# A mixture of experts that streams its weights: w1 and w3 loaded in halves for every pair, the second pair by quarters, and a late gather spread otherwise

## The reference

```python
def hier_moe(h, w_grp, b_grp, w_exp, b_exp, w1, w3, w2):
...
    w = pg_top * pe_top / jnp.sum(pe_top, axis=-1, keepdims=True)
    eid = g_sel * EXP_PER_GROUP + e_sel
    combine = jnp.sum(jax.nn.one_hot(eid, N_EXPERTS, dtype=f32) * w[..., None], axis=1)
    hid = jax.nn.silu(jnp.einsum('td,edf->tef', t, w1)) * jnp.einsum('td,edf->tef', t, w3)
    hid = hid * combine[..., None].astype(hid.dtype)
    out = jnp.einsum('tef,efd->td', hid, w2)
```

## Time and profile before

| | us |
|---|---|
| median of 3 runs | 1208.77 (1208.54 to 1209.69) |
| the profiled execution | 1207.29 |
| its span | 1205.5 |
| PE busy | 1173.3 (97%) |
| DVE busy | 700.5 (58%) |
| ACT busy | 379.0 (31%) |
| read from HBM | 334.97 MB |

### The profile page before, as it was taken

One profiled execution on the slowest core, in us unless ns is written; L12 is line 12 of the kernel. 1 busy time (PEld: TensorE's weight loads), 2 busy tenths in 40 slices (PEclk: granted clock), 3 DMA queues, 4 the chain that ended last, 5 costly groups with the idle time before them and its releaser, 6 DMA issues.

```text
span 1205.5 us, 18956 instructions
## 1 busy us (share of the span) xinstructions
PE 1173.3 (97%) x7316; PEld 886.3 (74%) x7316; DVE 700.5 (58%) x1024; ACT 379.0 (31%) x406; POOL 44.9 (4%) x53
## 2 busy tenths in 40 slices
PE   8999999999999999999999999999999999999995
PEld 8888888888888888888898888655555454545552
DVE  5778555556566767676886656444444444434445
ACT  5444433334444353543434543100101110000103
POOL 1000001001002022000000000000000000000002
PEclk9999999999999999999999999999999999999998
DMA  8665565765855555455664896999999999999996
GB/s 301 194 194 189 180 201 177 203 198 176 215 171 158 169 174 162 153 174 178 204 211 116 277 403 259 350 417 432 431 432 432 430 432 429 434 431 431 425 418 247
DMA packets 161707, 337.70 MB, mean 280 GB/s; under 512 B 13552, under 2 KB 139648, under 8 KB 148352
## 3 DMA queue, kind: packets, MB, share of 16 engines
q1 hardware_dynamic: 154544, 335.69, 75.8%
q10 hardware_dynamic: 7120, 1.42, 0.6%
HBM read 334.97 MB, written 2.12 MB: 280 GB/s over the span
## 4 chain that ended last, share of the span: by engine, by line
PE 82%; DMA 14%; DVE 1%; issue 1%; SPq 0%; ACT 0%; POOL 0%; POOLq 0%; DVEq 0%; ACTq 0%
PE ps L1056 20%; PE ps L1405 14%; DMA w_b<-in_w_dram 14%; PE ps L1086 12%; PE ps L1059 10%; PE ps L1089 6%; PE ps L1214 4%; PE ps L1437 4%; PE ps L1216 2%; PE ps L1446 2%; PE ps L1339 1%; PE ps L1447 1%; PE ps L1031 1%; PE ps L1178 0%; DMA xin<-in_x_dram 0%
## 5 line engine op out<-in xcount | busy, mean ns | idle before, releaser
L1533 DVE TENSOR_TENSOR wsplit<-wraw,wsplit 128x2048 fp32r<-128x2048 f32 x119 | 273.6, 2299 | 176.2 <-ACT wsplit L724 176.1
L724 ACT ACTIVATE wsplit<-wraw 128x2048 fp32r<-128x2048 f32 x119 | 228.1, 1917 | 368.3 <-PE ps L1059 194.1
L1056 PE MATMUL ps<-act_split,wsplit 128*128 128x512 f32 x1024 | 323.2, 397 | 0.0
L1405 PE MATMUL ps<-w_a,xe_a 128*64 128x256 f32 x960 | 219.8, 385 | 12.5 <-DMA w_b<-in_w_dram 12.2
L1059 PEld LDWEIGHTS ps<-act_split,wsplit 128*128 128x128 f32 x1024 | 192.4, 188 | 45.4
L1405 PE MATMUL ps<-w_b,xe_b 128*64 128x256 f32 x960 | 219.9, 385 | 0.0
L1405 PEld LDWEIGHTS ps<-w_a,xe_a 128*64 128x64 f32 x960 | 129.8, 138 | 98.1 <-DMA w_b<-in_w_dram 21.0
L1059 PE MATMUL ps<-act_split,wsplit 128*128 128x256 f32 x1024 | 201.3, 278 | 0.0
L1086 PE MATMUL ps<-wsplit,act_split 128*128 128x512 f32 x608 | 191.9, 397 | 0.0
L1056 PEld LDWEIGHTS ps<-act_split,wsplit 128*128 128x128 f32 x1024 | 156.4, 189 | 0.9 <-issue 0.4
L1089 PEld LDWEIGHTS ps<-wsplit,act_split 128*128 128x128 f32 x608 | 114.2, 188 | 26.9
(11 more groups left out here) (315 smaller groups left out, 1127.3 us busy)
## 6 DMA issues: line engine op xcount, KB each, us to landing
wraw<-in_w_in_dram SPq DMA_DIRECT2D x88, 1024.0 KB, 5.1
w_a<-in_w_dram SPq DMA_DIRECT2D x37, 2048.0 KB, 15.4
w_b<-in_w_dram SPq DMA_DIRECT2D x37, 2048.0 KB, 19.5
wraw<-in_w_out_dram SPq DMA_DIRECT2D x16, 1024.0 KB, 6.5
w_a<-in_w_dram SPq DMA_DIRECT2D x14, 1024.0 KB, 12.7
w_b<-in_w_dram SPq DMA_DIRECT2D x14, 1024.0 KB, 15.1
wraw<-in_w_branch_m_dram SPq DMA_DIRECT2D x8, 1024.0 KB, 5.1
wraw<-in_w_branch_a_dram SPq DMA_DIRECT2D x8, 1024.0 KB, 5.2
```

Of the source, the lines that this page charges most:

```text
L724: act.activation(wsplit[:, q % 2, :, 0], wraw[:, q % RAW], ACT.Copy).then_inc(rounded, 1)
L1056: pe.matmul(banks[b], w[:, k, 0, b * P:(b + 1) * P], act_of(q, k), start=first and k == 0, stop=False)
L1405: last = pe.matmul(ps[b * SLOTS:(b + 1) * SLOTS, 2 * w, 0:FF], operands[b][:, k], w13[b][:, w, k], start=k == 0, stop=k == DC - 1)
L1533: dve.tensor_tensor(wsplit[:, q % 2, :, 1], wraw[:, q % RAW], wsplit[:, q % 2, :, 0].bitcast(F32), ALU.subtract).then_inc(split, 1)
```

## The change

SP loads w1 and w3 of pairs 2 to 13 in halves of 1.05 MB, each after the part that used it, so eight loads a pair instead of four. Pair 1's come in quarters of 0.52 MB, 16 of them, released at the middle and the end of each of pair 0's parts (a new semaphore `mid_parts` in place of `first_quarter`). Each part on PE waits for its own half. PE's loop over pairs of pairs has its first pass written out.

The late gather's banks stand otherwise between pair 0's parts: one bank after each of the first two parts, two after each of the others, and the last two behind the turn, where it was 2, 2, 2, 1 and one behind the turn. On ACT the eviction of bank 6 moves behind the copy of the turned tile, and on DVE `up(0)` moves ahead of bank 5.

```diff
-                    for w, w_v in enumerate((w1_v, w3_v)):
-                        parts_done(i, 2 * w + 1)
+                    for part in range(PARTS):
+                        w, h = divmod(part, 2)
+                        ks = slice(h * PART_K, (h + 1) * PART_K)
+                        parts_done(i, part)
                         for b in range(2):
-                            sp.dma_start(w13[b][:, w], w_v[:, ds(i * 2 + b, 1)]).then_inc(w13_loaded[w][0], 16)
+                            sp.dma_start(w13[b][:, w, ks], (w1_v, w3_v)[w][:, ds(i * 2 + b, 1), ks]).then_inc(w13_loaded[w][h], 16)
...
-                sp.wait_ge(first_quarter, chunks)
-                for b in range(2):
-                    load_steps(b, 2 + b, 0, 0, DC // 4, w13_loaded[0][0])
-                parts_done(1, 0)
-                for b in range(2):
-                    load_steps(b, 2 + b, 0, DC // 4, DC // 2, w13_loaded[0][0])
-                for part in range(1, PARTS):
-                    parts_done(1, part)
-                    for b in range(2):
-                        load_part(b, 2 + b, part)
+                for part in range(PARTS):
+                    w, h = divmod(part, 2)
+                    for quarter in range(2):
+                        if quarter == 0:
+                            sp.wait_ge(mid_parts, (chunks - 1) * PARTS + (part + 1))
+                        else:
+                            parts_done(1, part)
+                        first = (2 * h + quarter) * (DC // 4)
+                        for b in range(2):
+                            load_steps(b, 2 + b, w, first, first + DC // 4, w13_loaded[w][h])
...
-                    gathered(1, (2, 4, 6))
+                    gathered(1, (2, 4))
                     turn_hidden(0)
+                    gathered(1, (6,))
...
-                    second_halves = {0: 32, LAST - 1: 96, LAST: 128}.get(i, 64) if isinstance(i, int) else 64
-                    quarters = 32 if w == 0 and not (isinstance(i, int) and i == 0) else 0
-                    pe.wait_ge(w13_loaded[w][h], second_halves if h else i * 32 + (32 + quarters))
+                    quarters = 0 if isinstance(i, int) and i == 0 else 32
+                    pe.wait_ge(w13_loaded[w][h], i * 32 + (32 + quarters))
...
-                        if isinstance(i, int) and i == 0 and part == 0 and k == DC // 4 - 1:
-                            last.then_inc(first_quarter, 1)
+                        if isinstance(i, int) and i == 0 and k % (DC // 2) == DC // 4 - 1:
+                            last.then_inc(mid_parts, 1)
...
-                hidden(0, 0, (xg[:, :, 0:SLOTS], xe_first), [[lambda js=js: gather_late(js)] for js in ((0, 1), (2, 3), (4, 5), (6,))])
+                hidden(0, 0, (xg[:, :, 0:SLOTS], xe_first), [[lambda js=js: gather_late(js)] for js in ((0,), (1,), (2, 3), (4, 5))])
                 turn(0)
-                gather_late((7,))
+                gather_late((6, 7))
...
-                with pe.Fori(0, N_PAIRS // 2 - 2) as j:
+                hidden_and_scatter(1, 0)
+                rows(0, 1, 1)
+                hidden_and_scatter(2, 1)
+                rows(1, 2, 0)
+                with pe.Fori(1, N_PAIRS // 2 - 2) as j:
...
                 make_x2(*late_chunks[0])
+                up(0)
+                starts_at = starts_of(1, 0)
                 gathered(1, (5,))
                 make_x2(*late_chunks[1])
-                up(0)
-                starts_at = starts_of(1, 0)
                 gathered(1, (7,))
```

More of the change, by code:

```diff
@@ L359, in layer @@
                              "hidT_ready", "ye_summed", "ye_ready"))
-        first_quarter = sem("first_quarter_of_w1_used")
+        mid_parts = sem("first_pair_half_parts_used")
         tile_summed, tile_added, tile_turned, tile_copied = (sem(n) for n in (
@@ L1470, in experts @@
                     pair_in_chunks(0, 0, 0)
-                    with pe.Fori(0, N_PAIRS // 2 - 2) as j:
+                    pair_in_chunks(1, 0, 1)
+                    pair_in_chunks(2, 1, 0)
+                    with pe.Fori(1, N_PAIRS // 2 - 2) as j:
                         pair_in_chunks(j * 2 + 1, j, 1)
```

## The result

| | before | after |
|---|---|---|
| median of 11 runs each, taken side by side | 1208.77 us | 1212.51 us |
| ratio, 95% interval | 1 | 1.0027 [1.0020, 1.0035] |
| the profiled execution (span) | 1207.29 (1205.5) | 1212.51 (1210.5) |
| PE busy | 1173.3 | 1173.7 |

The change is slower by 3.3 us (by the ratio), where no change was forecast (1209.6, up to 1211.9). Measured a second time it took 1211.24 us, ratio 1.0020 [1.0011, 1.0028]. Both lie on the slower side. PE has the same work and the same bytes are read; what grew is waiting.

What follows compares the result with a forecast made beforehand. The prediction took the weights' byte stream to bound the kernel from about 800 us. Start -1.6, gather +0.1 and halves +2.3 summed to +0.8 us: 1209.6 us forecast as median, no change, with 1207.7 to 1211.9 holding 8 in 10.

Steps and rivals of the forecast that it cites:

- The end is set by the byte stream: Experts' stage from about 800 us: every us by which the weight stream shifts is a us of the end.
- if PE and not the stream sets the last pairs: Last pairs of experts: a sign that would show the prediction wrong; no size given.
- PE's first loop pass is written out, with the same matmuls: PE's loop over pairs: writing out the first pass leaves the matmuls the same; no cost in the sum.
- Start, "1.6 us gained": Queue gaps at 745 to 785 us: earlier issues give back 1.6 of about 10 us lost, at most 2.9.
- At the 412 GB/s of a stretch of such quarters: Second pair's w1 and w3: quarters flow at 412 GB/s, so 8.39 MB are through at about 768.4 us.
- Pieces ran at 342 GB/s here: Third pair's w2 in eight pieces: at 342 GB/s from 771.3 us, its 4.19 MB end at 783.6.
- the gate that doesn't move: Fourth pair's w2: still issued at 800.85 us, after PE finishes pair 1's rows, which limits the start's gain.
- Halves, "loss 2.3 us": Pairs 3 to 13 under a full queue: 8 KB rows run slower than 16 KB rows, 2.3 us lost (1.5 to 3.0).
- They are slack behind the stream, and cost and gain nothing: PE's ten waits for weights: halves only move them to other places; size zero.
- The gather's order: Late gather between pair 0's parts: the new order costs 0.1 us, between 0 and 1.0.
- B: Rival, 13%: each load has its own price under a full queue, 1216.1 us; also slower if the start gains nothing.
- the deciding 423: Pairs 3 to 13: the rate in GB/s at which 3.9 us of loss makes the change slower by 2.4 us.

Runs made afterwards that it cites:

- e1: The change with PE's loop kept as before, its first pass not written out: 1210.24 us, ratio 1.0007 to the kernel before.
- e2: The kernel before with only PE's first loop pass written out: 1208.96 us, ratio 0.9998.
- e13: The kernel before with four extra unused 16 KB copies, each in one row (one packet): 1209.45 us, ratio 1.0005.
- e8: The change with all six passes of PE's loop written out instead of one: 1212.60 us, ratio 1.0036 to the kernel before.
- e5: The kernel before with the second pair's quarters, the gather's new order and halves for pair 2 alone, loop kept: 1207.77 us, ratio 0.9993.
- e4: The kernel before with only the second pair's quarters and the gather's new order; pairs 2 to 13 whole, loop kept: 1208.17 us, ratio 0.9994.
- e12: e5 with w2 of the third pair in two pieces of 1024 columns per expert instead of four of 512: 1208.41 us, ratio 0.9993 to before.
- e3: The kernel before with only w1 and w3 of pairs 2 to 13 loaded by halves: 1209.99 us, ratio 1.0009.
- e9: e5 with PE's first loop pass written out: 1209.09 us, ratio 1.0003 to the kernel before.
- e14: The kernel before with four extra unused 16 KB copies, each in 16 rows (16 packets): 1208.66 us, ratio 1.0001.
- e7: The kernel before with whole w1 and w3 loads of pairs 2 to 13 each cut into two of 64 partitions: 1509.36 us, ratio 1.2326.
- e6: The changed kernel measured and profiled once more, nothing altered: 1211.24 us, ratio 1.0020 to the kernel before.

## Why the prediction was wrong

- **"The end is set by the byte stream"**: right on the whole. It was read as bytes per us alone. Two things between bytes and the end were not in the sum: the last engine's lag (1.9 of the 3.6 us in the profiled change), and in some executions PE's clock. The sign "if PE and not the stream sets the last pairs" came in e1, e2 and e13, but not in the profiled change.
- **"PE's first loop pass is written out, with the same matmuls"**, costed at nothing: **this step failed**. Five pairs of kernels give -0.2, 1.1, 1.2, 1.0 and about 2.0 us, some 1 us in the mean, and in the change itself 1.6 to 2.4. The matmuls are the same; the code isn't. With the loop kept (e1) the change stands at 1.0007, which is +0.8 us, as in the sum; that the tenth agrees is luck, since e1's interval is 1.1 us to either side and PE, not the stream, set the end of its profile. What exactly the pass costs by stays open. Its code packets add nothing here (they do in e8), and the change's lag begins before them, with a slow issue on SP that only kernels with written-out code show.
- **Start, "1.6 us gained"**: mis-sized. In bytes e5 gained 0.98 and the change 0.59; in time e4 and e5 gained 0.7 and 0.8. Two terms in it were wrong. "At the 412 GB/s of a stretch of such quarters": they ran at 383, and 8.39 MB were through 24.9 us after the first load, not 22.4 (before 25.9). "Pieces ran at 342 GB/s here": that window of before held the last of the second pair's 8 KB rows beside the 2 KB rows of the pieces. With those gone earlier, the pieces stood alone, at 250 to 289. Moving the loads ahead took away the bytes that had filled the pieces' stretch. The releases, and the gate that doesn't move, were right to 0.15 us.
- **The Trainium skill's rule against the quarters.** Under a full queue the quarters of 0.52 MB ran at 383 GB/s, 89% of 431. The Trainium skill, "DMA: Bandwidth & Descriptors", section "Bandwidth", asks for 1 MiB for three quarters of peak; this row does not agree, the pieces of the same size in 2 KB rows (250, with a share of 0.92) do, and e12's pieces of 1.05 MB in 4 KB rows reach 389. So in these rows the length of a row counts more than the size of a load: at one size, 0.52 MB, rows of 4 KB ran at 383 and rows of 2 KB at 250 to 289, and at one length of row, 4 KB, twice the size gave 389 for 383. (w1 and w2 also lie differently in HBM, which no run changes.)
- **Halves, "loss 2.3 us"**: right. 2.28 us in the profiled bytes; by ratios e3 +1.1, e1 over e5 +1.7, the change over e9 2.0 to 2.9. (The prediction calls 2.3 "more than twice" 1.2; it is a little under twice.)
- **"They are slack behind the stream, and cost and gain nothing"**: the total rose (12.2 us before, 16.3 after, 13.0 in e1), and the kind changed, as the clock shows. By how much it moves a median isn't settled: e1 was PE-bound in its profile and still only 1.0007.
- **The gather's order**: at nothing or 0.1, and e4, that has it, is not slower.
- **Rivals.** B's price for each load (7.3 us) did not come: 429 GB/s is above the deciding 423. Its second clause, slower if the start gains nothing, is nearest to what came. Summed from the experiments: -0.8 + 2.0 + 1.0 = +2.2 us, against 2.4 and 3.3 measured; with the 1.6 to 2.4 that the pass costs in the change itself, 2.8 to 3.6.

## What to carry to other kernels

A window's rate is the rate of what was in it: before carrying it over, look whether the change leaves the same mix of rows there. In a stream that sets the end, measure landings too, since a load's last mark, and not the mean of its 16, releases the consumer. Finer loads belong only where the queue runs dry: e5, with halves in the one pair that needs them, keeps the gain without the price of the other eleven, though here that is less than can be measured.

## What was not expected of the hardware

- Longer waits of PE went with more time at the lower clock than the same time in short ones: behind a wait of 3.1 us the next 32 matmuls took 9.67 us for 7.02 (e1), and the time at the lower clock was 3.4 us in e14 (14.9 us of waiting in ten waits), 6.8 before, 10.2 in the change and 17.1 in e1 (13.0 us in six waits).
- Loads of 64 partitions stream at 241 GB/s instead of 431, though both halves of the partitions stand in the queue (e7).
- One issue by SP of a 0.52 MB piece took 1.5 to 2.3 us in the five profiles with quarters, w2 in eight pieces and code written out, and 0.8 to 1.0 in the three with the loop kept; by what is open.
- Landings can stay 2.1 to 2.8 us behind the bytes (expert b's loads in the change) for a stream of 360 us, once they have fallen behind: a full queue doesn't even them out. From the first of a load's 16 marks to the last it was 1.8 us in the mean before, and 3.2 to 3.4 in the change and in e6, in every stretch of 40 us from 790 to 1090.
